# Expert rows of 8 KB, gathered four at a time, and strips in place of diagonals

## The reference, cut to what matters

```python
qry = (xb @ w_query).reshape(blk, PEER_HEADS, 2, PEER_HALF)        # 8 heads, two halves
s = jnp.einsum('thpd,pkd->thpk', qry, sub_keys)                    # 128 keys for each half
sv, si = lax.top_k(s, 16)
cand = sv[:, :, 0, :, None] + sv[:, :, 1, None, :]                 # 16 x 16 pairs
best, pos = lax.top_k(cand..., 16); gate = softmax(best)           # eidx: 16 experts of 16384
u = expert_u[eidx]; v = expert_v[eidx]                             # two rows of 1024 each
act = gelu(einsum('td,thed->the', xb, u))
out = einsum('the,thed->td', gate * act, v)
```

## Time and profile before

| | us |
|---|---|
| median of 3 runs | 2301.08 (2298.81 to 2303.27) |
| the profiled execution, its time | 2301.28 |
| its span, first to last instruction | 2299.5 |

### The profile page before, as it was taken

One profiled execution on the slowest core, in us unless ns is written; L12 is line 12 of the kernel. 1 busy time (PEld: TensorE's weight loads), 2 busy tenths in 40 slices (PEclk: granted clock), 3 DMA queues, 4 the chain that ended last, 5 costly groups with the idle time before them and its releaser, 6 DMA issues.

```text
span 2299.5 us, 22838 instructions
## 1 busy us (share of the span) xinstructions
PE 1826.6 (79%) x6222; PEld 1033.5 (45%) x6222; DVE 1365.9 (59%) x3289; ACT 466.6 (20%) x1134; POOL 1165.0 (51%) x1148
## 2 busy tenths in 40 slices
PE   4998989888899998989876767686767776657676
PEld 2776678787763743444332323232323332223232
DVE  3442432376536565676566765676667578876764
ACT  1212443211000312121221211222121112111111
POOL 1000000000010377777767777777777777777775
PEclk9999999789799999999988888897879797878888
DMA  7326431000060899999989999999999999999997
GB/s 266 137 105 187 149 108 46 10 1 1 32 232 0 296 409 388 370 409 387 367 319 359 368 356 374 366 374 373 381 365 372 380 360 357 365 349 354 360 366 270
DMA packets 175122, 636.28 MB, mean 277 GB/s; under 512 B 22130, under 2 KB 22178, under 8 KB 174493
## 3 DMA queue, kind: packets, MB, share of 16 engines
q0 software_dynamic: 154128, 564.09, 65.8%
q1 hardware_dynamic: 20928, 71.36, 8.8%
HBM read 628.85 MB, written 7.56 MB: 277 GB/s over the span
## 4 chain that ended last, share of the span: by engine, by line
PE 47%; DVE 18%; issue 13%; DMA 10%; POOL 8%; ACT 4%; DVEq 0%; POOLq 0%; ACTq 0%; SPq 0%
PE abank L596 17%; PE fsum L948 14%; PE dbank L596 8%; DMA arena<-in_eu,small 7%; DVE arena L1400 6%; PE dbank L948 6%; POOL arena L331 5%; POOL arena L337 3%; DMA arena<-in_wstream 2%; DVE arena L1185 1%; ACT arena L436 1%; ACT arena L364 1%; PE dbank L631 1%; DVE arena L1340 1%; DVE arena L1201 1%
## 5 line engine op out<-in xcount | busy, mean ns | idle before, releaser
L1400 DVE CUSTOM_DVE_ANT_0 arena<-arena 128x1024 f32<-128x1024 f32 x520 | 626.9, 1225 | 377.5 <-DMA arena<-in_eu,small 363.3
L948 PE MATMUL dbank<-arena 128*128 128x512 f32 x1024 | 510.3, 662 | 228.1 <-ACT arena L549 228.1
L337 POOL DMA_INDIRECT arena<-in_ev,small x520 | 577.5, 1111 | 158.5 <-issue 148.7
L331 POOL DMA_INDIRECT arena<-in_eu,small x520 | 551.0, 1060 | 195.1 <-issue 125.9
L948 PE MATMUL fsum<-arena 128*128 128x512 f32 (+1 forms) x1056 | 511.6, 647 | 142.6 <-ACT arena L549 130.8
L596 PE MATMUL abank<-arena 128*128 128x256 f32 (+5 forms) x2080 | 448.6, 375 | 21.4 <-DMA arena<-in_wstream 7.9
L948 PEld LDWEIGHTS dbank<-arena 128*128 128x128 f32 x1024 | 216.0, 215 | 522.4 <-issue 420.7
L948 PEld LDWEIGHTS fsum<-arena 128*128 128x128 f32 (+1 forms) x1056 | 212.5, 204 | 437.6 <-issue 350.0
L596 PEld LDWEIGHTS abank<-arena 128*128 128x128 f32 (+2 forms) x2080 | 354.4, 192 | 115.6 <-issue 23.8
L596 PE MATMUL dbank<-arena 128*128 128x128 f32 (+9 forms) x1072 | 225.0, 372 | 8.0 <-ACTq L473 2.9
L596 PEld LDWEIGHTS dbank<-arena 128*128 128x128 f32 (+3 forms) x1072 | 164.5, 204 | 66.6 <-issue 50.1
(11 more groups left out here) (267 smaller groups left out, 1197.4 us busy)
## 6 DMA issues: line engine op xcount, KB each, us to landing
arena<-in_wstream SPq DMA_DIRECT2D x124, 512.0 KB, 4.6
arena<-in_eu,small POOLq DMA_INDIRECT x520, 6.2
arena<-in_ev,small POOLq DMA_INDIRECT x520, 6.3
arena<-in_x POOLq DMA_DIRECT2D x2, 2048.0 KB, 20.1
arena<-in_wout SPq DMA_DIRECT2D x1, 4096.0 KB, 17.2
arena<-in_sdel POOLq DMA_DIRECT2D x1, 2048.0 KB, 9.1
out_deltas<-arena POOLq DMA_DIRECT2D x1, 2048.0 KB, 8.5
arena<-mod POOLq DMA_DIRECT2D x4, 512.0 KB, 16.1
```

The costliest lines, as they stand in the source:

```text
L331: pool.indirect_dma_start(uring[j], None, I["eu"], bass.IndirectOffsetOnAxis(cur[:, a, j:j + 1], 0)).then_inc(u_in[j], 16)
L337: pool.indirect_dma_start(vring[j], None, I["ev"], bass.IndirectOffsetOnAxis(cur[:, a, j:j + 1], 0)).then_inc(v_in[j], 16)
L948: last = pe.matmul(fsum[n % 2][g][0:cols_, :], diag[:, j, 0:cols_], vring[j][:, g * 512:(g + 1) * 512], start=False, stop=False, skip_grou ...
L1400: TTR(uring[j], uring[j], x, 1.0, 0.0, ALU.mult, ALU.add, act8[:, a, j:j + 1]).then_inc(u_used[j], 1)
```

## The change

The two expert tables become one, `euv`, with rows of 8 KB: u, then v. A gather no longer takes one slot of 128 tokens but four slots of 32 tokens: partition 32k + m holds token 32j + m with slot 4k + kb. Four gathers (j = 0 to 3) make a quad, so a head has four quads (kb = 0 to 3), and there are 520 gathers in 130 quads. One ring of 7 slots of 8 KB per partition takes the place of two of 8 slots of 4 KB.

For this, indices and gates must be spread from token-major to the new layout: PE does that with columns of the identity (`select`), and ACT copies it out (`egs`). The h2 of each group of 32 tokens is repeated four times down the partitions (`replicate`: 8 groups of four matmuls per tile, evicted by ACT). DVE makes E4g, the gate of each partition times a pattern with a one where the column is the partition's token modulo 32 (`gated_units`, once for a head). After GELU of the four dots ACT scales four blocks of E4g of 128x32 by it, and PE multiplies each with the v half of its gather into 32 partitions of `fsum`, so the four gathers of a quad fill four strips. The matmuls on the first 512 columns are all queued before those on the second, and only the latter free the ring's slots.

The search is cut into four pieces, one after each quad's dots, and runs two heads ahead. The sample's 8 heads are searched at once, as 64 rows; its two quads go between tiles 2 and 3, each with 8-column stationaries into one strip. There is one pair of `fsum` banks: PE waits at each tile's start until ACT has copied the old tile out. Hardware loops are gone; all is written out.

```diff
-N_SEARCH = 27
 NKEY = 128
-SLOTS = 8
+SLOTS = 7
+NQ = 4
...
-        uring = [at(CT0 + D * j, D) for j in range(SLOTS)]
-        vring = [at(GA0 + D * j, D) for j in range(4)] + [at(R0 + D * j, D) for j in range(4)]
+        ring = [at(CT0 + 2 * D * i, 2 * D) for i in range(SLOTS)]
+        sc = at(GA0, 2 * PH * NKEY)
+        rep = [at(WB0, D), at(WB0 + D, D), at(GA0 + 2 * D, D), at(GA0 + 3 * D, D)]
+        E4g = at(E0 + D, 2, 4 * NQ * 32)
-        fsum = [[ctx.enter_context(nc.psum_tensor(f"fsum{i}", [P, 512], F32)) for i in range(2)], dbank[0:2]]
+        fsum = [ctx.enter_context(nc.psum_tensor(f"fsum{i}", [P, 512], F32)) for i in range(2)]
...
+        UNITS = [(t, h) for t in range(NT - 1) for h in range(PH)] + [(NT, 0)] + [(NT - 1, h) for h in range(PH)]
+        QUADS = [(u, t, h, kb) for u, (t, h) in enumerate(UNITS) for kb in range(NQ if t < NT else 2)]
+        ORDER = [0, 1, 2, NT, NT - 1]
...
-            def fetch(r, a, idx):
-
-                later = not (isinstance(r, int) and r == 0)
...
-                for j in range(SLOTS):
-                    pool.indirect_dma_start(uring[j], None, I["eu"],
-                                            bass.IndirectOffsetOnAxis(cur[:, a, j:j + 1], 0)).then_inc(u_in[j], 16)
-                for j in range(SLOTS):
-                    if later:
-                        pool.wait_ge(v_used[j], r)
-                        pool.sem_inc(s.pool_turn, 1)
-                    pool.indirect_dma_start(vring[j], None, I["ev"],
-                                            bass.IndirectOffsetOnAxis(cur[:, a, j:j + 1], 0)).then_inc(v_in[j], 16)
-
...
+            pool.wait_ge(s.sc_ready, 4)
+            for q, (u, t, h, kb) in enumerate(QUADS):
+                if kb == 0:
+                    pool.wait_ge(s.egs_ready, u + 1)
+                    if t < NT:
+                        idx = egs[:, u % 2, :].rearrange("p (j e k) -> p j e k", e=2, k=4)[:, :, 0, :]
+                        made = pool.tensor_copy(cur[:, u % 2, :].rearrange("p (j k) -> p j k", k=4), idx)
+                    else:
+                        made = pool.tensor_copy(cur[:, u % 2, 0:8], egs[:, u % 2, 0:8])
+                    made.then_inc(s.cur_ready, 1)
+                    pool.wait_ge(s.cur_ready, u + 1)
+                for j in range(NQ):
+                    if turn(q, j):
+                        pool.wait_ge(ring_used[slot(q, j)], turn(q, j))
+                    c = 4 * j + kb if t < NT else 4 * kb + j
+                    pool.indirect_dma_start(ring[slot(q, j)], None, I["euv"],
+                                            bass.IndirectOffsetOnAxis(cur[:, u % 2, c:c + 1], 0)).then_inc(ring_in[slot(q, j)], 16)
...
+            best_exp(1)
+            select(0)
+            replicate()
...
-            def weigh(r, a, base):
-
-                act.wait_ge(u_used[SLOTS - 1], r + 1)
-                A(act8[:, a, :], act8[:, a, :], ACT.Gelu).then_inc(s.gelu_ready, 1)
-                act.wait_ge(s.w_ready, r + 1)
-                for j in range(SLOTS):
-                    if not (isinstance(r, int) and r == 0):
-                        act.wait_ge(v_used[j], r)
-                    A(diag[:, j, 0:base.shape[1]], base, ACT.Copy, scale=w8[:, a, j:j + 1]).then_inc(s.diag_ready, 1)
...
+            for q, (u, t, h, kb) in enumerate(QUADS):
+                ahead = u + 2 < len(UNITS)
+                if ahead and kb == (3 if t < NT else 1):
+                    best_exp(u + 2)
+                act.wait_ge(s.dots_done, NQ * (q + 1))
+                step(A(gel[:, q % 2, :], dot[:, q % 2, :], ACT.Gelu), s.gelu_done)
+                if kb == 0:
+                    act.wait_ge(s.E4g_ready, u + 1)
+                if q >= 2:
+                    act.wait_ge(ring_used[slot(q - 2, NQ - 1)], turn(q - 2, NQ - 1) + 1)
+                for j in range(NQ):
+                    if t < NT:
+                        c0, n = 32 * (NQ * j + kb), 32
+                    else:
+                        c0, n = NB * (NQ * kb + j), NB
+                    A(S[:, q % 2, j, 0:n], E4g[:, u % 2, c0:c0 + n], ACT.Copy, scale=gel[:, q % 2, j:j + 1]).then_inc(s.diag_ready, 1)
+                if kb == 0 and u + 1 < len(UNITS):
+                    select(u + 1)
+                if t == 0 and h < 4:
+                    m = 4 * h + kb
+                    b = aring.to_read()
+                    step(A(qryL[:, m, :], b[:, 0:SEQ - P], ACT.Copy))
+                    step(A(qs[:, m % 2, NB * (m // 2):NB * (m // 2) + NB], b[:, SEQ - P:TOK - P], ACT.Copy), s.aring_free)
...
+                if ended(q, 1) is not None:
+                    norm(2 * (NT + 1) + ORDER.index(ended(q, 1)))
+                if last_quad(q):
...
+            def select(u):
+
+                pe.wait_ge(s.eg_ready, u + 1)
+                b = aring.to_fill()
+                if UNITS[u][0] < NT:
+                    for j in range(NQ):
+                        for k in range(4):
+                            last = pe.matmul(b[32 * k:32 * k + 32, 8 * j:8 * j + 8], ident[:, 32 * j:32 * j + 32], pick[:, :, 4 * k:4 * k + 4],
+                                             start=True, stop=True, skip_group_check=True)
...
+            def replicate(t):
+
+                for j in range(NQ):
+                    for g in range(2):
+                        b = aring.to_fill()
+                        for k in range(4):
+                            last = pe.matmul(b[32 * k:32 * k + 32, :], ident[:, 32 * j:32 * j + 32], h2[:, t, g * 512:(g + 1) * 512],
+                                             start=True, stop=True, skip_group_check=True)
+                        last.then_inc(s.aring_full, 1)
...
+            for q, (u, t, h, kb) in enumerate(QUADS):
+                if first_quad(q) and q:
+                    pe.wait_ge(s.f_out, ORDER.index(t))
                 for g in range(2):
-                    pe.matmul(fsum[n % 2][g][:, :], zeros[:, :], consts[:, 0:512], start=True, stop=False, skip_group_check=True)
-
-            def add_round(n, r, cols_):
-                for j in range(SLOTS):
-                    pe.wait_ge(s.diag_ready, r * SLOTS + (j + 1))
-                    pe.wait_ge(v_in[j], r * 16 + 16)
+                    for j in range(NQ):
+                        if g == 0:
+                            pe.wait_ge(s.diag_ready, NQ * q + j + 1)
+                        v = ring[slot(q, j)][:, D + 512 * g:D + 512 * g + 512]
+                        if t < NT:
+                            last = pe.matmul(fsum[g][32 * j:32 * j + 32, :], S[:, q % 2, j, :], v,
+                                             start=first_quad(q), stop=last_quad(q), skip_group_check=True)
+                        else:
+                            last = pe.matmul(fsum[g][0:NB, :], S[:, q % 2, j, 0:NB], v,
+                                             start=first_quad(q) and j == 0, stop=last_quad(q) and j == NQ - 1, skip_group_check=True)
+                        if g == 1:
+                            last.then_inc(ring_used[slot(q, j)], 1)
+                if kb == 0 and u + 1 < len(UNITS):
+                    select(u + 1)
+                if t == 0 and h < 4:
+                    query(4 * h + kb)
+                if t < NT - 1 and kb == 2 and h in SC_AT:
...
-            def add_round(n, r, cols_):
-                for j in range(SLOTS):
-                    pe.wait_ge(s.diag_ready, r * SLOTS + (j + 1))
-                    pe.wait_ge(v_in[j], r * 16 + 16)
-                        last = pe.matmul(fsum[n % 2][g][0:cols_, :], diag[:, j, 0:cols_], vring[j][:, g * 512:(g + 1) * 512],
-                                         start=False, stop=False, skip_group_check=True)
-                    last.then_inc(v_used[j], 1)
...
+            def search(u, piece):
+
+                t, h = UNITS[u]
...
+            def gated_units(u):
+
+                dve.wait_ge(s.egs_ready, u + 1)
+                if u >= 2:
+                    dve.wait_ge(s.diag_ready, NQ * ([x[0] for x in QUADS].index(u - 1)))
+                if UNITS[u][0] < NT:
+                    g = egs[:, u % 2, :].rearrange("p (j e k) -> p j e k", e=2, k=4)[:, :, 1, :]
+                    TT(E4g[:, u % 2, :].rearrange("p (j k m) -> p j k m", k=4, m=32), bc(g, 3, 32),
+                       bc(bc(consts[:, C_E4:C_E4 + 32], 1, 4), 1, 4), ALU.mult).then_inc(s.E4g_ready, 1)
...
+            for u in range(2):
+                for piece in range(4):
+                    search(u, piece)
+            gated_units(0)
+            for q, (u, t, h, kb) in enumerate(QUADS):
+                if q >= 2:
+                    dve.wait_ge(s.gelu_done, q - 1)
+                if t == NT and kb == 0:
+                    dve.wait_ge(s.h2sb_ready, 1)
+                for j in range(NQ):
+                    if t < NT and first_quad(q):
+                        dve.wait_ge(s.rep_ready, 8 * t + 2 * j + 2)
+                    dve.wait_ge(ring_in[slot(q, j)], 16 * (turn(q, j) + 1))
+                    uh = ring[slot(q, j)][:, 0:D]
```

(37 more changed lines are left out.)

545 lines of the change are left out of this document (225 added, 320 removed).

## The result

The changed kernel took 2408.39 us (median of 4 runs, 2399.51 to 2410.69), the kernel before 2302.18 (2298.81 to 2312.47): ratio 1.0446, 95% interval 1.0404 to 1.0489. It is 4.5% slower, where 0.8% was forecast. The profiled execution took 2407.84 us around a span of 2406.0.

A forecast was written before the change was run, and what follows sets the result against it. A loop of release and landing over seven slots, 11.5 us per quad, was to bind above DMA's 10.1: 800 + 16 x 11.3 + 113 x 11.5 + 22 + 16, 2320 us; own range 2275 to 2377, full range 2140 to 2430.

The forecast's parts named there:

- rival (c): Thin queue: engines restart cold, landing nearer the loaded 6.2 us than 4.3; loop 12.4, 2422 us, slower; chance 0.11.
- Gathers, DMA rate: 520 gathers of 1 MB at 1.39 us of POOL each; 8 KB rows move at 416 GB/s, 10.1 us per quad.
- (d): Rows cut to 4 KB on issue: gather issue 2.1 us instead of 1.0, loop 12.6, 2445 us; chance 0.07.
- (e): PE strips don't overlap: five instructions of 1.71 us before the first release, loop 16.6 us, about 2895 us; chance 0.04.
- Release: From a quad's last landing through dot, GELU, S and half-clock matmuls to the freed slot: 5.6 us; POOL starts 0.1 later.
- (a): PE's clock stays up or releases come early: loop under 10.1 us, DMA binds, 2154 us, faster; chance 0.24.
- Landing of the critical gather: A quad's last gather, which waits for a slot, lands 5.6 us after issue into an empty queue, 5.7 to its dot.
- First quads: First 16 quads, with 16 query weight tiles of 0.5 MB beside them: DMA binds at 11.3 us each.
- Start: Two searches and other work before the first gather put it at 786.5 us; first quad complete at 800 us.
- boundaries: Between tiles, PE waits for fsum copies and replicated halves; with the sample quads the sum is 22 us, between 8 and 30.
- Tail: After the last landing, the remaining PE work, copies, normalising operations and output take 16 us.
- rival (b): Part of the landing overlaps: 1 MB lands in 4.6 us, loop 10.4, 2196 us, faster; chance 0.11.

The follow-up runs named there:

- e_split: Changed kernel with each slot filled by two gathers of 4 KB rows (u and v from tables of their own) instead of one of 8 KB: 2413.74 us.
- e_depth: Changed kernel without dots or weighing of rows, a fixed number of gathers in flight: landing 5.4 us alone, 5.5 with two, 9.9 with four, 17.1 with seven.
- e_ring8: Changed kernel with eight slots instead of seven from the 73rd gather on: 2238.99 us.
- e_depth3: Changed kernel without dots or weighing, other numbers in flight: landing 7.7 us with three, 12.2 with five; batches of four from empty, period 14.5 us on the mean.
- e_each: Changed kernel with GELU, S and both matmuls after each dot instead of each fourth, seven slots: 2166.15 us.
- e_warm6: Changed kernel with six matmuls that compute nothing behind each quad outside the query stage, seven slots: 2382.58 us.

## Why the prediction was right in its sign and short in its size

The direction and the place held: slower, because a ring of seven slots with releases by quads closes a loop that is longer than the transfers. The direction was close to a coin toss all the same: I gave 0.49 to slower and 0.44 to faster. The measured 2408 us lies outside the forecast's own range of 2275 to 2377, and only the reach for rival (c) took it in. By the terms of its sum:

- *Gathers, DMA rate.* Right: 1106 ns a gather, rows not cut (the issue costs what one of e_split's 4 KB rows costs, 1082 and 1152 ns), 418 to 421 GB/s at best where I had 416. The mean of 1106 is made of 0.94 us and of issues that begin inside a dot. Rivals (d) and (e) are out: the strips of a quad took 4.26 us, not 8 x 1.71.
- *Release.* Right: 1.9 + 1.71 + 1.71 + 0.25 + 0.1 is 5.67, measured 5.77. The half clock was right too, so (a) did not come.
- *Landing of the critical gather.* This is the term that failed. I took "5.6, and 0.05 to the dot, say 5.7", the landing of one gather into an empty queue. That price itself is right, or a little high: 5.4 us alone in e_depth. In the changed kernel the way from issue to dot is 6.25 us in the median and 6.59 on the mean, 0.9 more than the 5.7. I had priced an empty queue and an undisturbed issue, and both were wrong. In 47 of 109 distances the issue falls into one of DVE's dots and is stretched to 1.54 us on the mean, where I had added 0.1; without the stretch the landing there is that of a lone gather (5.46). In the other 62 the engines hardly ever run dry, though I had said they would: in 57 of these two gathers are still under way at the issue (in 43 of the 47 it is one), three more follow, and the dot comes after 6.82 us. Over all quads the fourth dot starts 4.0 us behind the third, where 2.5 suffice in e_ring8. By its number that is rival (c), to which I gave 0.11: its loop of 12.4 and 2422 us lie nearest to what came. Its mechanism, engines that restart cold, the runs show only for the gather behind a restart (3.4 us in e_depth3 where 2.5 suffice): a lone gather restarts them too, and lands in 5.4.
- *First quads.* I had DMA bind there at 11.3 us. They took 12.39: the same loop holds while weights ride beside it. The price for DMA alone was good (11.2 in e_depth with four in flight), but e_each, with the loop cut, still takes 11.8 there, so about half of the 1.1 us is the loop's.

The dots that bound these stretches, from the timeline of the changed kernel:

```profile
796.82 1.23 DVE L1432 CUSTOM_DVE_ANT_0 arena<-arena 128x1024 f32<-128x1024 f32 x1 [1.26 <-DMA arena<-in_euv,delta]
...
995.13 1.23 DVE L1432 CUSTOM_DVE_ANT_0 arena<-arena 128x1024 f32<-128x1024 f32 x1 [3.22 <-DMA arena<-in_euv,delta]
...
2391.06 1.23 DVE L1432 CUSTOM_DVE_ANT_0 arena<-arena 128x1024 f32<-128x1024 f32 x1 [3.69 <-DMA arena<-in_euv,delta]
```

The terms of the sum make 2318.3, not 2318.6. Start: 796.8 for 800, -3. First sixteen: 198.3 for 180.8, +17.5. The boundaries cost about 12 us for 22, -10: the five distances at them are together that much longer than five others. 5.9 of it are in the first quad behind the sample's, whose critical gather waits 12.7 us for the strips of the sample instead of 5.8. The 113 quads: 1395.9 less those 12 is 12.25 each for 11.5, +84. Tail 14.9 for 16, -1. Together +87.6, from 2318.3 to 2406.0.

The Trainium skill (DMA: Bandwidth & Descriptors, the anatomy of one DMA) gives a DMA from GpSimd about 2.0 us plus its bytes over 436 GB/s. For 1 MB that makes an estimate of 4.4 us, and e_depth has 5.4 with nothing beside it. The measurement decides: rival (b), which leaned that way, is out for this kind of gather.

Whether what I foresaw as evidence came: the single wait of POOL per quad did (859 us for fsum), the rate did (341 GB/s at a share of 0.90), and the clock near 0.6. Search pieces delayed no more than two of 109 fourth dots; the others waited for their gather. The landings "at 5.5 to 5.8" did not come, and I had named no evidence for that case.

What stays open is the 6.82 us of the quads in which the issue is short. e_warm6 issued the critical gather 1 us earlier and it still landed 4.0 us behind the third. With two in flight and nothing behind them (e_depth) that distance is 2.9 us in the median (2.5 to 3.7 in most), so the three gathers that GpSimd issues right behind the critical one are a candidate for the rest. It wasn't tried, nor was a kernel that keeps the issues clear of the dots.

## What to carry to other kernels

When transfers are made larger inside the same memory, count the slots, not the bytes: a group size of four over seven slots leaves one transfer of each group waiting for the whole group, and that one loop set the time (14.97, 12.07, 10.7, 9.95 us for 6, 7, 8, 9 slots). Release by the slot even where the work per slot gets dearer: PE did 320 us more and the kernel came out 10% faster (2166 us, against 2414 for e_split on the same chip). And read a DMA share of 0.9 together with its GB/s: 340 at 0.9 is a queue with two or three gathers in it, which stops in some rounds and dips in others, 420 at 1 is a full one. And look at what DVE does when GpSimd issues on the path: a gather that starts inside a dot pays for the rest of the dot (1.54 us instead of 0.94 here).

## What the runs showed of the hardware

- An indirect gather of 128 rows of 8 KB: 5.4 us from issue to landing when alone, 2.48 us each when five or more are in flight; two in flight move 351 GB/s, three 395 (e_depth, e_depth3).
- After a gap the engines move 160 to 310 GB/s for about 1.5 us, and the second gather behind a gap still takes 3.4 us in the median (2.8 to 3.9 in most, e_depth3).
- Issuing such a gather costs GpSimd 0.94 us at least and 1.1 on the mean, for rows of 4 KB as of 8 KB. What makes the mean is DVE: an issue that begins inside a dot (two operands of 128x1024 in SBUF) ends about 0.82 us after the dot does, 141 of 147 times; a dot that begins after the issue doesn't lengthen it (157 such issues from the 81st gather on, none over 0.97 us). The kernel before shows the same (199 of 204), and in e_depth, which has no dots, the mean issue is 0.97 us.
- The kernel before differed by 9% between chips (2511 and 2302 us), while all its runs on one chip lay within 1.5%. e_split, bound by the loop, shows no such difference (2413.74 us there, 2408 to 2414 for the changed kernel elsewhere).
